# Mixer A value products: two query tiles at once with stationary values in high and low parts, and the attention steps one step sooner

## The reference

```python
def attend(qb):
    s = jnp.einsum('bqhcd,bshcd->bhcqs', qb, k).astype(jnp.float32) * scale
    p = jax.nn.softmax(s, axis=-1)
    p = p[:, :, 0] - lam[None, :, None, None] * p[:, :, 1]
    return jnp.einsum('bhqs,bshe->bqhe', p.astype(v.dtype), v)
...
oa = rms_norm(oa, subln_l) * (1.0 - lam_init)
o = jnp.concatenate([oa.reshape(b, n, A_V) * jax.nn.silu(ga), ...], axis=-1)
```

## Time and profile before

| what | before |
|---|---|
| time, median of 3 runs | 1274.22 us (1273.89 to 1274.27) |
| profiled execution: time / span | 1274.88 us / 1273.1 us |
| TensorE busy | 1232.3 us, 97% |
| VectorE busy | 768.6 us, 60% |
| ScalarE busy | 601.0 us, 47% |
| GpSimd busy | 259.2 us, 20% |
| granted TensorE clock, mean | 0.99 |

### The profile page before, as it was taken

How to read it: one execution, slowest core, us unless ns; L and a number is a source line. 1 busy time by engine, 2 the same in 40 slices (tenths; PEclk the granted TensorE clock), 3 DMA queues, 4 the chain that set the end, 5 groups by cost and what they waited for, 6 DMA issues and landing times.

```text
span 1273.1 us, 17812 instructions
## 1 busy us (share of the span) xinstructions
PE 1232.3 (97%) x6751; PEld 992.4 (78%) x6751; DVE 768.6 (60%) x1187; ACT 601.0 (47%) x1259; POOL 259.2 (20%) x440
## 2 busy tenths in 40 slices
PE   4899999999999999999999999999999999999994
PEld 4456888888888888788787878888787878778883
DVE  4255578677586776654636464554546564869683
ACT  5232325645555455454555555554646645212223
POOL 2111023022030130222222121212223312110102
PEclk9799999999999999999999999999999999999997
DMA  9998332222221223312221222222224423746454
GB/s 336 385 380 310 98 108 75 63 70 71 75 95 47 79 87 80 95 51 81 58 82 58 63 77 66 75 65 73 68 70 131 137 66 108 246 142 229 158 177 182
DMA packets 130070, 156.51 MB, mean 123 GB/s; under 512 B 8273, under 2 KB 97009, under 8 KB 129217
## 3 DMA queue, kind: packets, MB, share of 16 engines
q1 hardware_dynamic: 116400, 109.65, 26.3%
q0 software_dynamic: 13584, 45.72, 11.6%
HBM read 144.18 MB, written 11.16 MB: 122 GB/s over the span
## 4 chain that ended last, share of the span: by engine, by line
PE 93%; DMA 2%; SPq 2%; DVE 1%; issue 1%; ACT 0%; POOL 0%; ACTq 0%; DVEq 0%; POOLq 0%
PE z_ps L650 25%; PE z_ps L652 24%; PE z_ps L651 24%; PE ring L742 5%; PE ring L777 4%; PE ring L842 4%; PE ring L672 2%; PE ring L846 2%; SPq L616 1%; PE ring L652 1%; PE ring L651 1%; PE ring L849 1%; PE ring L650 1%; DMA gate_b<-gate_rows 1%; DMA ada_raw<-in_w_ada_dram 1%
## 5 line engine op out<-in xcount | busy, mean ns | idle before, releaser
L650 PE MATMUL z_ps<-w_hi,xt_hi 128*128 128x512 f32 x1360 | 563.2, 414 | 4.7 <-DVE xt_lo L1269 3.2
L652 PE MATMUL z_ps<-w_hi,xt_lo 128*128 128x512 f32 x1360 | 532.3, 391 | 0.0
L651 PE MATMUL z_ps<-w_lo,xt_hi 128*128 128x512 f32 x1360 | 531.7, 391 | 0.0
L925 ACT ACTIVATE w_hi<-w_raw 128x512 fp32r<-128x512 f32 x272 | 170.7, 628 | 341.5 <-PE z_ps L652 319.7
L1275 DVE TENSOR_TENSOR w_lo<-w_raw,w_hi 128x512 fp32r<-128x512 f32 x272 | 196.7, 727 | 200.5 <-ACT w_hi L925 200.2
L650 PEld LDWEIGHTS z_ps<-w_hi,xt_hi 128*128 128x128 f32 x1360 | 256.1, 188 | 64.9 <-issue 18.4
L652 PEld LDWEIGHTS z_ps<-w_hi,xt_lo 128*128 128x128 f32 x1360 | 255.7, 188 | 56.2
L651 PEld LDWEIGHTS z_ps<-w_lo,xt_hi 128*128 128x128 f32 x1360 | 257.1, 189 | 39.7
L1362 DVE TENSOR_REDUCE small<-s_sb 128x2 f32<-128x1536 f32 (+1 forms) x60 | 88.3, 1472 | 22.4 <-ACT s_sb L925 21.2
L1036 ACT ACTIVATE s_sb<-s_sb,small 128x768 f32<-128x768 f32 (+1 forms) x120 | 97.9, 820 | 2.7 <-DVE small L1362 2.7
L1695 POOL TENSOR_TENSOR sg<-sg,zs 128x128 f32<-128x128 f32 (+1 forms) x60 | 38.3, 638 | 282.7 <-DVE sg L1345 282.0
(11 more groups left out here) (167 smaller groups left out, 1352.9 us busy)
## 6 DMA issues: line engine op xcount, KB each, us to landing
w_raw<-in_w_in_dram SPq DMA_DIRECT2D x186, 256.0 KB, 3.2
ada_raw<-in_w_ada_dram SPq DMA_DIRECT2D x64, 512.0 KB, 12.2
w_raw<-in_w_out_dram SPq DMA_DIRECT2D x64, 256.0 KB, 3.5
gate_raw<-in_w_ada_dram POOLq DMA_DIRECT2D x12, 1024.0 KB, 7.2
w_raw<-in_w_in_dram POOLq DMA_DIRECT2D x22, 256.0 KB, 6.2
o_spill<-row_st POOLq DMA_DIRECT2D x14, 320.0 KB, 3.5
row_st<-o_spill POOLq DMA_DIRECT2D x14, 320.0 KB, 3.5
x_sb<-in_x_sample_dram SPq DMA_DIRECT2D x4, 1024.0 KB, 10.2
```

Of the source, the lines that this page charges most:

```text
L650: pe.matmul(out, hi_l, hi_r, start=start, stop=False)
L651: pe.matmul(out, hi_l, lo_r, start=False, stop=False)
L652: return pe.matmul(out, lo_l, hi_r, start=False, stop=stop)
L925: return act.activation(out, in_, ACT.Copy, **kw)
```

## The change

In mixer A only:

- `T(t)` is copied out as a high part by ScalarE and a low part by VectorE (`pt_los`), as in mixer B. Its bank is now freed by VectorE.
- `V(1)` and `V(3)` each make two query tiles at once with the values stationary: per key tile one product of 512 columns and one of 256. `V(2)` and `V(4)` are gone. The result stands transposed, so ScalarE and VectorE add its two parts into `o_back` and a new piece `B(1)`, `B(3)` transposes two blocks back. `V(0)` has the map stationary: one product of 256 and one of 128 columns.
- VectorE makes a low part of the values (`v_lo`). The squares, roots and gated rows of two tiles come after each `B`.
- A new table `STEPS_A` puts `QK`, `S`, `T`, `V(0)` one step sooner than `STEPS`. `gate_inverse` stays in steps 4 to 8.

```diff
+STEPS_A = {
+    1: [("O", -1)], 2: [("QK", 0)], 3: [("S", 0)], 4: [("S", 1)], 5: [("T", 0)], 6: [("S", 2), ("V", 0)], 7: [("T", 1)],
+    8: [("S", 3)], 9: [("T", 2)], 10: [("S", 4), ("V", 1)], 11: [("T", 3)], 12: [("B", 1)], 13: [("T", 4)], 14: [("V", 3)],
+    15: [("B", 3)],
+}
-LAST_STEPS = dict(STEPS)
-LAST_STEPS[10] = [("T", 2), ("S", 4)]
-LAST_STEPS[11] = [("V", 2), ("T", 3)]
-LAST_STEPS[12] = [("V", 3), ("T", 4)]
-LAST_STEPS[13] = [("V", 4)]
+LAST_STEPS = dict(STEPS_A)
+LAST_STEPS[9] = [("T", 2), ("S", 4)]
+LAST_STEPS[10] = [("V", 1), ("T", 3)]
+LAST_STEPS[11] = [("B", 1), ("T", 4)]
+LAST_STEPS[12] = [("V", 3)]
+LAST_STEPS[13] = [("B", 3)]
...
-LAST_PLACES = {11: [1, 3, 4], 12: [2, 3, 4], 13: [3], 14: [3, 4]}
+LAST_PLACES = {10: [1, 3, 4], 11: [1, 3, 4], 12: [3], 13: [2], 14: [3, 4]}
...
+            if group_kind(a) == "D":
+                return [(n + j // 4, (t - 1) % 2, j, m, 0, True) for j, m in ((0, 4), (4, 2))]
...
-                    if group_kind(a) == "D":
-                        ins = pe.matmul(bank[:, 0:DH], pt_f[:, keys], v_f[:, vt, :],
-                                        start=(j == 0), stop=last)
+                    if group_kind(a) == "D" and t == 0:
+                        pe.matmul(bank[:, 0:2 * DH], pt_hi[0][:, keys], v_hl[vh][:, vt, :],
+                                  start=True, stop=False, skip_group_check=True)
+                        ins = pe.matmul(bank[:, 0:DH], pt_lo[0][:, keys], v_hl[vh][:, vt, 0:DH],
+                                        start=False, stop=True, skip_group_check=True)
                         continue
...
+            def step_b(a, t):
+
+                n = TURN[("B", a, t)]
+                wait_free(pe, TURN[("V", a, t)])
+                bank = claim(n)
+                for c_ in range(2):
+                    ins = transpose(bank, P * c_, o_back[:, c_, :])
+                filled(ins, n)
...
-                    if group_kind(a) == "D":
-                        copy(pt_f[:, keys], RB(n)[:, col:col + P * w]).then_inc(free_sem(n), 1)
-                    else:
-                        copy(pt_hi[c_][:, keys], RB(n)[:, col:col + P * w]).then_inc(pt_hi_done, 1)
+                    copy(pt_hi[c_][:, P * j0:P * (j0 + w)], RB(n)[:, col:col + P * w]).then_inc(pt_hi_done, 1)
...
+            def o_rows(a, t):
+
+                n = TURN[("B", a, t)]
+                wait_outputs(act, a, t - 1)
+                wait_full(act, n)
+                copy(o_sum[:, :, 0:DH], RB(n)[:, 0:2 * P].rearrange("p (c d) -> p c d", c=2)).then_inc(free_sem(n), 1)
+                wait_free(act, n)
+                for u in (t, t + 1):
+                    o_squares(a, u)
```

More of the change, by code:

```diff
@@ L112, in heads, with outputs_of @@
     return 2 if group_kind(a) == "G" else 1
+def outputs_of(kind, a, t):
+    if group_kind(a) != "D":
+        return []
+    return [0] if kind == "V" and t == 0 else [t, t + 1] if kind == "B" else []
 def steps_at(it, s):
@@ L121, in steps_at @@
         return [("QK", KV_IT, 0)] if s == KV_QK_STEP else []
[L122 removed]
+    for kind, t in (LAST_STEPS if it == OUT_IT else STEPS_A if group_kind(it - 1) == "D" else STEPS).get(s, []):
         a = it - 1
@@ L172, in pieces_at @@
             out[i * TILES // len(flat)].append(piece)
+        elif group_kind(it - 1) == "D" and (piece[0] in ("QK", "B") or piece[0] == "S" and piece[2] == 0):
+            out[3 if piece[0] == "S" else 2 + i].append(piece)
         elif piece[0] in ("V", "GT"):
@@ L503, in build, with o_slot @@
                         PT_BEFORE[(a_, t_)] = npt
-                        npt += len(t_parts(a_, t_)) if group_kind(a_) == "G" else 0
+                        npt += len(t_parts(a_, t_))
+        O_PART = {}
+        for a_ in range(G_IT, OUT_IT):
+            for t_ in (0, 1, 3) if group_kind(a_) == "D" else range(TILES):
+                O_PART[(a_, t_)] = len(O_PART) + 1
+        def o_slot(a, t):
+            return (t + 1) % 2 if group_kind(a) == "D" else t % 2
+        o_back = o_sum[:, :, DH:2 * DH]
         V_DONE, OG_DONE, G_DONE, ROW_DONE = [], [], [], []
@@ L832, in step_v @@
                 pe.wait_ge(v_lo_done, V_DONE[a])
-                for m, *_ in t_parts(a, t):
-                    wait_free(pe, m)
+                for u in (t, t + 1) if group_kind(a) == "D" and t else (t,):
+                    for m, *_ in t_parts(a, u):
+                        wait_free(pe, m)
                 bank = claim(n)
@@ L905, in between @@
                             step_gt(a, tile)
+                        elif kind == "B":
+                            step_b(a, tile)
                         else:
@@ L1041, in pt_his @@
                     wait_full(act, n)
-                    keys = slice(P * j0, P * (j0 + w))
-                    if group_kind(a) == "D":
-                        copy(pt_f[:, keys], RB(n)[:, col:col + P * w]).then_inc(free_sem(n), 1)
-                    else:
-                        copy(pt_hi[c_][:, keys], RB(n)[:, col:col + P * w]).then_inc(pt_hi_done, 1)
+                    copy(pt_hi[c_][:, P * j0:P * (j0 + w)], RB(n)[:, col:col + P * w]).then_inc(pt_hi_done, 1)
             def o_low(a, t):
                 n = TURN[("V", a, t)]
-                m = n_step(a, t)
+                low = RB(n)[:, :].rearrange("p (c u d) -> p c u d", c=2, u=2)[:, :, 1, :]
+                if group_kind(a) == "D" and t:
+                    if t > 1:
+                        wait_full(act, TURN[("B", a, 1)])
+                    elif a > D_IT:
+                        wait_full(act, TURN[("B", a - 1, 3)])
+                    wait_full(act, n)
+                    copy(o_back, low).then_inc(o_part, 1)
+                    return
                 if t >= 2:
@@ L1057, in o_low @@
                 wait_full(act, n)
-                h = heads(a)
                 if group_kind(a) == "D":
-                    copy(o_sum[:, t % 2, 0:DH], RB(n)[:, 0:DH]).then_inc(free_sem(n), 1)
-                    return
-                copy(o_sum[:, t % 2, 0:DH * h].rearrange("p (c d) -> p c d", c=h),
-                     RB(n)[:, 0:2 * DH * h].rearrange("p (c u d) -> p c u d", c=h, u=2)[:, :, 1, :]
-                     ).then_inc(o_part, 1)
+                    copy(o_sum[:, o_slot(a, t), 0:DH], RB(n)[:, DH:2 * DH]).then_inc(o_part, 1)
+                else:
+                    copy(o_sum[:, t % 2, :].rearrange("p (c d) -> p c d", c=2), low).then_inc(o_part, 1)
             def o_squares(a, t):
@@ L1150, in _ @@
                         exps(a, t)
-                    if kind == "V":
+                    if kind == "V" and t == 0:
                         o_squares(a, t)
@@ L1165, in _ @@
                             o_low(a, t)
-                        if a and t == TILES - 1:
-                            o_squares(a, t)
+                    elif kind == "B":
+                        o_rows(a, t)
                     elif kind == "O":
@@ L1562, in _ @@
                     for kind, a, t in old:
-                        if kind == "V":
-                            gated(a, t)
+                        for u in outputs_of(kind, a, t):
+                            gated(a, u)
                 if 0 < it <= OUT_IT:
@@ L1830, in _ @@
                         spill(a)
-                    if kind == "V" and t == TILES - 1:
-                        o_root(a, t)
+                    if kind == "B":
+                        for u in (t, t + 1):
+                            o_root(a, u)
                 late = [step for step in late if step[0] != "V" or step[2] < TILES - 1]
```

40 lines of the change are left out of this document (16 added, 24 removed).

## The result

The changed kernel takes **1282.38 us** (median of 6 runs, 1281.21 to 1283.77), the kernel before 1274.01 us in runs between them (6 runs, 1273.74 to 1274.27). The ratio is 1.0065, 95% interval 1.0052 to 1.0078: 8.4 us slower. The forecast was 3.6 us slower (1277.6), with a range up to 1281.5. The sign was right, the size was not. Run a second time, the changed kernel took 1282.41 us against 1274.77, ratio 1.0059 (1.0047 to 1.0072).

What follows compares the result with a forecast made beforehand. The prediction took TensorE's list, busy 97% of the span, as the bound. Saving 5.8 us against waits of 2.2, 3.5, 2.4 and 1.1 us gave +3.4 us, a median of 1277.6 us, range 1270.5 to 1281.5.

Steps and rivals of the forecast that it cites:

- What bounds it: Whole kernel: TensorE's list bounds the time, 93% of the chain; other engines' work costs nothing until TensorE waits for it.
- What TensorE saves: Mixer A's value products: 0.72 us saved per head, 5.8 us in eight heads; a double product takes 2.11 us.
- D0 to D5: Before S(4) in each of six heads: TensorE waits 0.36 us for T(2)'s low parts, 2.2 us in all.
- D7: Head D7: TensorE waits 2.4 us before S(4) and 1.1 us before T(4).
- D6, the step that failed: Head D6, which also splits row blocks: TensorE waits 3.5 us before S(4).
- The rival: More waits: lost cover at head ends, +3.5 us, 1281.1 us, or D6 waits 2 us longer; chance 0.12.
- Cost nothing: QK at step 2, B(1), B(3) and the z_ps copies at a head's end: no TensorE wait, 0.7 us cover left.
- No wait at all, faster: Rival: TensorE waits nowhere, -5.8 us, 1268.4 us; needs the first gated row or GpSimd's root sooner; chance 0.13.

Runs made afterwards that it cites:

- The control with both moves: Kernel before, with GpSimd's roots ahead of the gate products in every step and D6's row-block loads at the head of each step: 1274.63 us, ratio 1.0000.
- the run with the root first: Changed kernel with GpSimd's root of block 0 ahead of the gate products of its step: 1275.69 us, 1.0009 of the kernel before.
- the run with the loads of keys and values behind: Changed kernel with GpSimd's two loads of keys and values (step 5) behind that step's row-block load: 1280.99 us, ratio 1.0053.
- The two moves alone and together: Changed kernel with block 0's root ahead of gate products: 1275.69 us; with D6's row-block loads at head of step: 1277.12 us; with both: 1271.01 us.
- the second profile: Changed kernel run once more, unchanged: 1282.41 us, its profiled execution 1283.02 us.
- the sooner steps with the row blocks on time: Kernel before with mixer A's attention one step sooner, old value products, and D6's row-block loads at the head of each step: 1274.33 us, ratio 0.9996.
- the run with both moves: Changed kernel with block 0's root ahead of the gate products and D6's row-block loads at the head of each step: 1271.01 us, ratio 0.9968.
- two more edits: Changed kernel, root and row-block loads moved ahead, plus mixer A reciprocals and gate products a step sooner and T(4) at place 4 of step 11: 1270.00 us.
- four of 0.94 us: The 1270.0 us kernel with two more maxima of S(3) on VectorE in each of D1 to D4: 1273.69 us.
- the run with four long waits: The 1270.0 us kernel with three more maxima of S(3) on VectorE in each of D1 to D4: 1287.67 us, ratio 1.0102.

## Why the prediction was right in its sign and wrong in its size

**What bounds it.** Right as far as it goes: the time went with TensorE's list and its waits, and with its clock, of which the forecast says nothing. The control with both moves gained nothing before the change.

**What TensorE saves.** Forecast 0.72 us per head, measured 0.68 (heads 71.40 us apart without a wait, 72.08 before), 5.4 us in all in place of 5.8 if all eight save alike; from D6 to D7 it was only 0.44. A double product takes the 2.11 us of mixer B's (first product at 703.39, next projection product at 705.50). By the isolated gap that the Trainium skill gives in the page "TensorE: Matmul & The Clock Gate", section "Back-to-back issue gap", it would have been 1.95, an estimate from that page; the trace doesn't agree, here as before.

**D0 to D5.** Right: one wait each before `S(4)`, released by the low parts of `T(2)`, 0.34 us where 0.36 was worked out. The list from the gated row to the low parts ran without a gap, and the run with the root first showed that the 2.40 us behind GpSimd are the cause.

**D7.** Right: 2.39 for 2.4, and 0.86 before `T(4)` for 1.1. A wait of 0.20 before `O` was missing. The cause of the first is again the root: it fell to 0.33 with it.

**D6, the step that failed.** The forecast took over the gated row of D6 from the trace of before, as it had done for D2 "with everything up to the gated row as it was: the same pieces stand in front of it on all engines". In D6 that is false. The row blocks' loads stayed at their steps on GpSimd's list, behind the gate products, while the copies that stand in line behind them on ScalarE were wanted a step sooner. So a wait came before `S(3)`, 2.39 us, which the forecast had put at nothing. From there on it was right: from the first product of `S(3)` (982.15 before the change) to the free banks it has 12.58 us, measured are 12.48. The wait before `S(4)` was nevertheless 1.80 and not 3.5, because TensorE had lost 1.6 us at half clock on the way; at full clock it is 3.36, in the run with the loads of keys and values behind. So D6 lost 2.39 + 1.80 + 1.6 = 5.8 us where 3.5 was forecast. That the two waits alone make 4.2, near the 3.5, is chance. The rival had the place and about the price ("D6, whose row blocks come by DMA, waits 2 us longer"), at 0.12 with another case. The two moves alone and together, and the sooner steps with the old products, show that both the root and the loads hold this head.

**The clock, a term that was missing.** The sum priced a wait at its own length. In the profiled execution the stretch at half clock behind 979.18 cost nothing beyond that, since a wait of 3.4 us stood behind it and became shorter by as much. Where nothing hides it so, a stretch of 3.4 us costs 1.5 to 1.6 us, as in D7 of the second profile. The median of the changed kernel lies 1.2 us above its profiled execution, and such stretches are a likely reason. That is argued, not shown: the other executions have no trace.

**The sum with its measured terms.** -5.4 + 2.0 (six waits) + 4.2 (D6) + 2.4 + 0.9 + 0.2 (D7) + 1.6 (half clock) = +5.9 us, against 6.3 in the span. Of the 0.4 us between them 0.24 is the smaller saving from D6 to D7; the rest is not located. Forecast and measured time are 4.8 us apart. Of these, 2.9 are terms: 2.3 in D6, 0.4 of saving and 0.4 not in the sum, less 0.2 for the other waits. 1.2 us lie between the profiled execution and the median of after, and 0.7 us is what the forecast had taken off because the profiled execution of before lay that much above its median.

**Cost nothing.** Right, and now shown: the sooner steps with the row blocks on time take 1274.33 us, so queries and keys at step 2 and the first scores cost nothing. That `B` and the copies of `z_ps` at a head's end cost nothing is shown by the run with both moves, where TensorE has no wait in D0 to D6. TensorE waits at no first projection product of these heads; the wait of 0.95 us before the final projection (1092.67) was there before (1086.17).

**Rivals.** "No wait at all, faster", 1268.4 us, is where the kernel can be brought: the forecast said that it needs the root sooner, "and the change alters neither". With two moves on GpSimd and two more edits it is 1270.0 us, 4.8 us under the kernel before.

## What to carry to other kernels

When work is moved sooner, list for every engine what did not move with it. Here the loads of the row blocks and the reciprocals kept their steps, and the root, which moved, kept its place behind a gate product. In lists that are worked off in order this made TensorE wait. A sign of it stood in the trace of before: ScalarE already waited for the row blocks there, 1.46 and 1.23 us (973.04 and 979.00), without harm.

Judge a move by the distance between two fixed places, and not by the wait at the second alone. A wait is also as long as TensorE is early: it shrank from 3.36 to 1.80 us because TensorE was slow on the way to it, and stayed at about 2 us when one of its two causes was removed, though each move had taken 1.2 to 1.5 us off VectorE's list. Try the pair before dropping either.

And price a long wait of TensorE above its length, unless a later wait hides the rest: here four of 0.94 us cost about 1 us each, four of 2.70 us 4.4 each.

## What the runs showed of the hardware

Behind a wait of TensorE its granted clock can fall to 0.50 for some microseconds, though TensorE is busy again. The fall came 0.2 to 1.6 us after the end of the wait in nine of ten cases, and 0.3 us ahead of it in one (D4 of the run with four long waits); the stretches lasted 3.4 us, in that one case 6.8. At 2.70 us this followed in four of four, and cost 1.7 us each. Between 2.19 and 2.53 us it followed six times of nine: behind 2.39 and 2.53 in D6 (before `S(3)`) and 2.19 and 2.23 (before `S(4)`) it did, behind 2.39 before `S(3)` in the run with the root first it did not; behind 2.37 to 2.39 in D7 it followed in two profiles of four. At 1.84 us and below none followed. The length alone doesn't decide, since behind the 3.36 us of D6 the windows show 1.00. What decides was not found.

The Trainium skill, page "TensorE: Matmul & The Clock Gate", section "HAM oscillation — how this bites in real kernels", tells of waits for DMA of about 3 to 5 us between bursts of products, behind each of which the next burst starts at half clock. The traces here agree only in part: waits of 2.19 to 2.70 us, shorter than those, were followed in ten cases of thirteen, and the one of 3.36 us was not.
